# Where TensorE waits for u at the first down unit: one wait, or one per use

## The chip, the cores and the metric

One core of a Trainium2 chip runs the whole program. The metric is the device time of one execution in microseconds. The kernel before took 2634.83 us (median of 3 runs, 2634.37 to 2636.46).

## The reference

A streaming encoder trunk of two layers, for 512 prompt tokens and 32 sample tokens (544 columns in all), model width 1024. Each layer is FFN, middle part, FFN. What matters here is the FFN:

```
h = rmsnorm(x, norm_g[0]) * (1 + mod[:, 1]) + mod[:, 0]
x = x + 0.5 * mod[:, 2] * swiglu(h, w_up1, w_down1)

def swiglu(h, w_up, w_down):
    a, b = jnp.split(h @ w_up, 2, axis=-1)
    return (jax.nn.silu(a) * b) @ w_down          # w_up 1024 x 5632, w_down 2816 x 1024
```

Below, `u` is silu(a) * b. The middle part (pooling, retention, gates, output projection) is not touched. The vectors `mod` come from a product of the condition with `w_ada`, which the kernel spreads over the FFN stages.

## The kernel before, in words

**Data.** Everything is stored with features on the 128 partitions and the 544 tokens in the free dimension, cut into two column halves of HT = 272, called `hf` 0 and 1. Every fp32 operand is held as a rounded part and a remainder (`u_hi`, `u_lo`; `w_hi`, `w_lo`), and `product` (L447) makes a product out of three matmuls for each block of 128 rows: hi*hi, hi*lo and lo*hi, all summed in one PSUM bank.

**The FFN on TensorE** (`ffn`, L564) is cut into two halves of the 2816 hidden rows, HK = 11 blocks each. A half has 11 up units and then KD = 8 down units. There are two FFNs in each of two layers, so 8 halves. An up unit (`block_unit`, L484; `first_unit` for the first of a half 0) makes `a` and `b` of one block of u: for each `hf` it runs two products of 8 row blocks, 48 matmuls, 96 for the unit. A down unit makes 128 of the 1024 output features from the 11 blocks of u: for each `hf` one product with nk = 11, so 33 matmuls, 66 for the unit. Down unit n sums into the pair of PSUM banks n % 2.

**What follows an up unit.** When the last matmul of a `hf` ends, ScalarE applies Silu to `a` (L855), VectorE multiplies by `b` (L1189), and `two_parts` (L1030) rounds the result into `u_hi` (L1032) and stores the remainder in `u_lo` (L1034). The last of these raises the semaphore `u_ready` by 1, in the order block 0 hf 0, block 0 hf 1, block 1 hf 0, and so on: 22 rises in a half. The tally `u_t` counts them on TensorE's side.

**What TensorE waits for at a down unit.** `begin_unit` (L436) waits for `w_split`, the weights of the unit; `take` (L440) for the bank pair, `acc_free`; and ahead of the 8 down units of a half there is one wait for all 22 rises of `u_ready`:

```
place += 2 * HK
u_t.step(2 * HK)
pe.wait_ge(u_ready, u_t.at())
for n in range(KD):
    begin_unit()
```

**Weights.** SyncE loads the weights of a unit into one of two buffers `raw`, in order, once the buffer's previous content has been split (`w_split`). ScalarE rounds them into `w_hi` (L784) and VectorE forms `w_lo` (`split`, L1040). Both have two buffers as well, so ScalarE rounds the weights of unit m + 2 after unit m has ended on TensorE. In VectorE's order of work the split for down unit 0 stands ahead of both column halves of the last up unit, and the split for down unit 1 stands behind the u of hf 1 and behind one share of the `w_ada` work.

**The w_ada work.** While chunks of it are left, VectorE runs `due` after each column half of an up unit and after each down unit: four multiply-adds with `w_ada` rows (L1065), whose loads GpSimd's queue issues when a buffer comes free. Every fourth time TensorE sums the result in 16 small matmuls (`mods`, L497, L507). At the last block of a half this work is there in four of the 8 halves (both of the first FFN of layer 0, the first half of its second FFN and the first half of layer 1's first FFN).

**After a down unit** VectorE adds the result to x (`update_x`, L1154). In the second half of an FFN ScalarE then squares x for the next norm.

Of the kernel before, what the change touches and what calls it, by code (L numbers as in the profile page):

```python
# [20 lines left out]
HK = FF // P // 2  # L21
# [84 lines left out]
def trunk_kernel(nc, x_prompt, x_sample, c_prompt, c_sample, cache_pool, state_ret, w_ada, b_ada,  # L106
# [4 lines left out]
    with ctx:  # L111
        def sb(name, shape, dt=F32, stack=ctx):
            return stack.enter_context(nc.sbuf_tensor(name, [P, *shape], dt))

        def sem(name):
            return ctx.enter_context(nc.semaphore(name))
# [28 lines left out]
        with ExitStack() as st:  # L145
            u_hi, u_lo = sb("u_hi", [HK, T], F32R, st), sb("u_lo", [HK, T], F32R, st)
# [51 lines left out]
        u_ready = sem("u_ready")  # L198
# [230 lines left out]
        def _(pe):  # L429
            unit, ada, pair0, pair1, squares, h0, h1, u_t, tails, yp_t, mask_t, y_t, gn_t, side_t, layers = \  # L430
# [5 lines left out]
            def begin_unit():  # L436
                pe.wait_ge(w_split, unit.at(1))
                unit.step()

            def take(p):  # L440
                pe.wait_ge(acc_free[p], pairs[p].at(1))

            def done(p, ins):
                ins.then_inc(acc_ready[p], 1)
                pairs[p].step()

            def product(out, ws, xs, nk):  # L447


                for kk in range(nk):  # L450
                    for n, (a, b) in enumerate(((0, 0), (0, 1), (1, 0))):
                        last = mm(out, ws(a, kk), xs(b, kk), start=(kk == 0 and n == 0),  # L452
                                  stop=(kk == nk - 1 and n == 2))
                return last

            def cols(hf):
                return slice(hf * HT, (hf + 1) * HT)

            def parts(hi, lo, hf):
                return lambda b, kk: (hi, lo)[b][:, kk, cols(hf)]  # L460

            def w_view(p, pattern, n, **sizes):
                return [t[p][:, 0:n].rearrange(pattern, **sizes) for t in (w_hi, w_lo)]

            def first_unit(p, place=None):

                begin_unit()
                w = w_view(p, "p (b k n) -> p b k n", SLOT, b=2, k=KD)
                take(0)
                take(1)  # L470
                for kk in range(KD):
                    hs[kk % 2].step()
                    pe.wait_ge(h_ready[kk % 2], hs[kk % 2].at())
                    for hf in range(2):
                        for b in range(2):
                            for n, (c, d) in enumerate(((0, 0), (0, 1), (1, 0))):
                                last = mm(acc[:, 2 * hf + b, 0:HT], w[c][:, b, kk, :], (h_hi, h_lo)[d][:, kk, cols(hf)],  # L477
                                          start=(kk == 0 and n == 0), stop=(kk == KD - 1 and n == 2))
                        if kk == KD - 1:
                            done(hf, last)  # L480
                            if place is not None:
                                mods(place[0], place[1] + hf)

            def block_unit(p, place=None):  # L484

                begin_unit()
                w = w_view(p, "p (b k n) -> p b k n", SLOT, b=2, k=KD)
                for hf in range(2):
                    take(hf)
                    for b in range(2):  # L490
                        last = product(acc[:, 2 * hf + b, 0:HT], lambda a, kk: w[a][:, b, kk, :],
                                       parts(h_hi, h_lo, hf), KD)
                    done(hf, last)
                    if place is not None:
                        mods(place[0], place[1] + hf)

            def mods(todo, place):  # L497

                n, behind = divmod(place - LATE - 3, 4)
                if behind or not 0 <= n < len(todo):  # L500
                    return
                ada.step(4)
                pe.wait_ge(ada_used, ada.at())
                c = todo[n][1]
                for g in range(2):
                    for b in range(4):
                        last = mm(mod_cols(c // CHUNKS, (c % CHUNKS) * 4 + b, 1)[:, 0, g:g + 1],  # L507
                                  ada_acc[n % 2][:, g, b * P:(b + 1) * P], const[:, K_ONE:K_ONE + 1],
                                  start=True, stop=True)
                last.then_inc(mods_summed, 1)  # L510
# [45 lines left out]
            for layer in range(DEPTH):  # L556
                pe.matmul(ps_misc[:, layer * 192:layer * 192 + R_ALL], rows_in[0:R_ALL, layer, 0, :],
                          ident[0:R_ALL, 0:R_ALL], is_transpose=True, start=True, stop=True)
                n = R_CACHE + (2 * KD if layer == 0 else 0)
# [4 lines left out]
            def ffn(todo):  # L564
                for half in range(2):
                    place = half * (2 * HK + KD)
                    for n in range(HK):
                        if half == 0 and n == 0:
                            first_unit(0, (todo, place))
                        else:  # L570
                            block_unit((half + n) % 2, (todo, place + 2 * n))
                    place += 2 * HK
                    u_t.step(2 * HK)
                    pe.wait_ge(u_ready, u_t.at())
                    for n in range(KD):
                        begin_unit()
                        w = w_view((half + 1 + n) % 2, "p (k n) -> p k n", HK * P, k=HK)
                        take(n % 2)
                        for hf in range(2):
                            last = product(acc[:, 2 * (n % 2) + hf, 0:HT], lambda a, kk: w[a][:, kk, :],  # L580
                                           parts(u_hi, u_lo, hf), HK)
                        done(n % 2, last)
                        mods(todo, place + n)

# [65 lines left out]
            def middle():  # L650
                for kind, n in MID:
# [14 lines left out]
                    elif kind == "v":  # L666
                        begin_unit()
                        w = w_view(slot, "p (k n) -> p k n", SLOT, k=KD)
                        for t in range(TOK):
                            p = (n * TOK + t) % 2  # L670
                            rows = P if t < JB else TS
                            take(p)
                            done(p, product(acc[0:rows, 2 * p, 0:256],
                                            lambda a, kk: (h_hi, h_lo)[a][:, kk, t * P:t * P + rows],
                                            lambda b, kk: w[b][:, kk, :], KD))
                    elif kind == "map":
                        begin_unit()
                        w = w_view(slot, "p (g n) -> p g n", 2 * P, g=2)
                        for e in range(2):
                            g = 2 * n + e  # L680
                            yp_t.step()
                            pe.wait_ge(yp_ready, yp_t.at())
                            take(e)
                            for hf in range(2):
                                last = product(acc[:, 2 * e + hf, 0:HT], lambda a, kk: w[a][:, e, :],
                                               lambda b, kk: (yp_hi, yp_lo)[b][:, g, cols(hf)], 1)
                            done(e, last)
                    elif kind == "head":
                        head(n)
                    elif kind in ("mean", "var"):  # L690
                        group_sum()
# [36 lines left out]
            for layer in range(DEPTH):  # L728
                column_sums(KD)
                if layer == 0:  # L730
                    direct_rows()
                ffn(moved(layer, 0))
                column_sums(KD)
                middle()
                column_sums(KD)
                ffn(moved(layer, 2))
# [696 lines left out]
```

## Time and profile before

| | |
|---|---|
| median of 3 runs | 2634.83 us |
| the profiled execution, its own time | 2635.26 us |
| its span in the trace | 2633.4 us |
| mean granted TensorE clock | 0.977 |
| PE busy | 2478.3 us (94%), 19084 matmuls |
| DVE busy | 1473.5 us (56%) |
| ACT busy | 745.4 us (28%) |
| POOL busy | 241.6 us (9%) |
| HBM traffic | 105 GB/s over the span |

PE is TensorE's matmuls, PEld its weight loads (which overlap them), DVE is VectorE, ACT ScalarE, POOL GpSimd, SPq SyncE's DMA queue. Matmuls are pipelined: two that follow each other start about 0.125 us apart though each is shown with 0.29 us, so rates are read from starts and from stretches, not from the duration of one. PEclk is the granted TensorE clock as a share of 2.4 GHz: 1.00 is 2.4 GHz and 0.50 is 1.2 GHz.

### The profile page before, as it was taken

The page shows a single profiled execution, that of the slowest core. Times are in us where ns is not written, and L with a number is a line of the kernel's source. Part 1 is how long each engine was busy: PE and PEld are TensorE (multiplying, and loading weights), DVE is VectorE, ACT ScalarE, POOL GpSimd, SP SyncE. Part 2 cuts the span into 40 slices and gives each one's busy share as a digit, 9 for nine tenths or more (in the row PEclk, how much of TensorE's full clock was granted, in tenths as well). Part 3 has the DMA queues.
Part 4 walks back from the last instruction along what each step waited for, and adds up shares of the span by engine and source line. Part 5 has one row for each costly group of instructions (what it writes and reads, how often), then busy time and mean ns, then how long its engine had stood idle before and what let it go on. Part 6 is the DMA issues. An engine that isn't in the chain of part 4 may idle for free.

```text
span 2633.4 us, 42638 instructions
## 1 busy us (share of the span) xinstructions
PE 2478.3 (94%) x19084; PEld 2412.5 (92%) x19084; DVE 1473.5 (56%) x2229; ACT 745.4 (28%) x892; POOL 241.6 (9%) x232
## 2 busy tenths in 40 slices
PE   7899999898899899999989999998989998999997
PEld 2899999888799899999989999998879998999997
DVE  1876776645745577534367667645555545434333
ACT  2311222433422431222241122234233234212222
POOL 1210111101000221000021001011000002000001
PEclk9899999999999999999999999999999998999998
DMA  6554654311123355332245455332112323323321
GB/s 203 182 156 136 174 163 126 100 51 53 55 73 105 96 152 158 99 97 76 77 121 168 143 163 164 101 92 78 42 47 73 94 77 87 83 75 106 82 67 56
DMA packets 401157, 279.91 MB, mean 106 GB/s; under 512 B 10090, under 2 KB 379218, under 8 KB 400846
## 3 DMA queue, kind: packets, MB, share of 16 engines
q1 hardware_dynamic: 379027, 204.73, 27.5%
q0 software_dynamic: 18432, 67.12, 8.4%
q10 hardware_dynamic: 3515, 5.34, 0.6%
q8 instruction: 150, 2.46, 0.4%
q14 instruction: 33, 0.27, 0.0%
HBM read 273.74 MB, written 3.40 MB: 105 GB/s over the span
## 4 chain that ended last, share of the span: by engine, by line
PE 87%; DVE 6%; ACT 4%; issue 1%; DMA 1%; POOL 1%; ACTq 0%; POOLq 0%; DVEq 0%
PE acc L452 76%; PE acc L477 3%; PE ps_mod L507 2%; PE acc L720 2%; ACT w_hi L784 1%; DVE w_lo L1043 1%; DVE rstd L1118 1%; PE ps_sum L605 1%; DMA ada_raw<-in_w_ada 1%; POOL h_lo L383 1%; DVE rstd L1310 1%; ACT h_hi L797 0%; PE ps_sum L540 0%; DMA x_in<-in_x_sample 0%; DVE tmp L1127 0%
## 5 line engine op out<-in xcount | busy, mean ns | idle before, releaser
L452 PE MATMUL acc<-h_hi,w_hi 128*128 128x272 f32 x3648 | 1055.2, 289 | 9.5 <-DVE q L1301 3.6
L452 PE MATMUL acc<-h_lo,w_hi 128*128 128x272 f32 x3648 | 1051.8, 288 | 0.0
L452 PE MATMUL acc<-h_hi,w_lo 128*128 128x272 f32 x3648 | 1051.4, 288 | 0.0
L1043 DVE TENSOR_TENSOR w_lo<-raw,w_hi 128x2048 fp32r<-128x2048 f32 x224 | 512.7, 2289 | 358.6 <-ACT w_hi L784 358.5
L452 PEld LDWEIGHTS acc<-h_hi,w_hi 128*128 128x128 f32 x3648 | 688.5, 189 | 12.8 <-issue 12.0
L452 PEld LDWEIGHTS acc<-h_lo,w_hi 128*128 128x128 f32 x3648 | 688.3, 189 | 0.0
L452 PEld LDWEIGHTS acc<-h_hi,w_lo 128*128 128x128 f32 x3648 | 686.9, 188 | 0.0
L784 ACT ACTIVATE w_hi<-raw 128x2048 fp32r<-128x2048 f32 x224 | 427.7, 1909 | 333.1 <-PE acc L452 223.3
L452 PE MATMUL acc<-u_hi,w_hi 128*128 128x272 f32 x1408 | 407.4, 289 | 14.2 <-DVE u_lo L1034 14.2
L452 PE MATMUL acc<-u_lo,w_hi 128*128 128x272 f32 x1408 | 408.8, 290 | 0.0
L452 PE MATMUL acc<-u_hi,w_lo 128*128 128x272 f32 x1408 | 408.0, 290 | 0.0
L855 ACT ACTIVATE acted<-acc 128x272 f32<-128x272 f32 x176 | 70.0, 398 | 848.2 <-PE acc L452 839.6
L1065 DVE SCALAR_TENSOR_TENSOR ada_acc<-ada_raw,c_by,ada_acc 128x512 f32<-128x512 f32 x448 | 307.5, 745 | 0.1
L1189 DVE TENSOR_TENSOR prod<-acted,acc 128x272 f32<-128x272 f32 x176 | 76.8, 436 | 395.2 <-ACT acted L855 395.0
L452 PEld LDWEIGHTS acc<-u_hi,w_hi 128*128 128x128 f32 x1408 | 268.8, 191 | 15.9 <-DVE u_lo L1034 15.9
L452 PEld LDWEIGHTS acc<-u_hi,w_lo 128*128 128x128 f32 x1408 | 268.7, 191 | 0.0
L452 PEld LDWEIGHTS acc<-u_lo,w_hi 128*128 128x128 f32 x1408 | 268.2, 190 | 0.0
L383 POOL TENSOR_TENSOR h_lo<-tmp,h_hi 128x544 fp32r<-128x544 f32 x56 | 84.4, 1510 | 1332.7 <-ACT h_hi L797 1332.5
L1159 DVE SCALAR_TENSOR_TENSOR x<-acc,coef,x 128x272 f32<-128x272 f32 (+2 forms) x288 | 99.2, 400 | 182.6 <-PE acc L452 172.2
L411 POOL DMA_DIRECT2D ada_raw<-in_w_ada x128 | 92.6, 723 | 709.6 <-DVE ada_acc L1065 696.5
L477 PE MATMUL acc<-h_hi,w_hi 128*128 128x272 f32 x192 | 61.7, 321 | 54.1 <-DVE h_lo L1144 44.0
L796 ACT ACTIVATE tmp<-x 128x544 f32<-128x544 f32 x56 | 36.7, 656 | 220.4 <-issue 197.8
(171 smaller groups left out, 2507.8 us busy)
## 6 DMA issues: line engine op xcount, KB each, us to landing
raw<-in_w_up SPq DMA_DIRECT2D x176, 512.0 KB, 5.3
ada_raw<-in_w_ada POOLq DMA_DIRECT2D x128, 512.0 KB, 4.1
raw<-in_w_in SPq DMA_DIRECT2D x72, 512.0 KB, 4.6
raw<-in_w_down SPq DMA_DIRECT2D x64, 384.0 KB, 4.2
raw<-in_w_down SPq DMA_DIRECT2D x64, 320.0 KB, 3.4
ada_raw<-in_w_ada SPq DMA_DIRECT2D x16, 512.0 KB, 4.6
raw<-in_w_o SPq DMA_DIRECT2D x32, 256.0 KB, 2.9
raw<-in_w_pool_out SPq DMA_DIRECT2D x16, 256.0 KB, 3.0
```

The costliest lines, as they stand in the source:

```text
L383: pool.tensor_tensor(h_lo[:, n, :], tmp[:, n % 2, :], h_hi[:, n, :].bitcast(F32), ALU.subtract)\
L411: pool.dma_start(ada_raw[slot][:, :, :], ada_source(l, c, kp)).then_inc(ada_landed[slot], 16)
L452: last = mm(out, ws(a, kk), xs(b, kk), start=(kk == 0 and n == 0), stop=(kk == nk - 1 and n == 2))
L477: last = mm(acc[:, 2 * hf + b, 0:HT], w[c][:, b, kk, :], (h_hi, h_lo)[d][:, kk, cols(hf)], start=(kk == 0 and n == 0), stop=(kk == KD - 1 ...
L507: last = mm(mod_cols(c // CHUNKS, (c % CHUNKS) * 4 + b, 1)[:, 0, g:g + 1], ada_acc[n % 2][:, g, b * P:(b + 1) * P], const[:, K_ONE:K_ONE + 1],
L720: last = mm(acc[:, 2 * b + hf, 0:HT], w[c][:, kk, b * P:(b + 1) * P], (m_hi, m_lo)[d][:, kk, cols(hf)], start=(kk == 0 and n == 0), stop=( ...
L784: act.activation(w_hi[p][:, :], raw[p][:, :], ACT.Copy).then_inc(w_rounded, 1)
L855: act.activation(acted[:, hf, 0, :], acc[:, 2 * hf, 0:HT], ACT.Silu).then_inc(acted_ok, 1)
L1043: dve.tensor_tensor(w_lo[p][:, :], raw[p][:, :], f(w_hi[p][:, :]), ALU.subtract).then_inc(w_split, 1)
L1065: last = dve.scalar_tensor_tensor(to[:, g, :], ada_raw[slot][:, e, :], by, to[:, g, :], ALU.mult, ALU.add)
L1159: last = dve.scalar_tensor_tensor(x[:, n, c:c + b - a], acc[:, 2 * p + hf, a:b], coef[:, s, 2, n, g:g + 1], x[:, n, c:c + b - a], ALU.mult ...
L1189: dve.tensor_tensor(prod[:, hf, 0, :], acted[:, hf, 0, :], acc[:, 2 * hf + 1, 0:HT], ALU.mult).then_inc(acc_free[hf], 1)
```

## The change

The one wait ahead of the down units goes. In the first down unit of each half (n == 0), `product` is handed the base value of `u_ready` and waits twice itself: at its first row block for all blocks of u but the last, of its own column half, and at its last row block for that block. The other seven down units have no wait for u, before as after.

```
-            def product(out, ws, xs, nk):
+            def product(out, ws, xs, nk, ready=None):
                 for kk in range(nk):
+                    if ready is not None and kk in (0, nk - 1):
+                        pe.wait_ge(u_ready, ready + (2 * kk if kk else 2 * nk - 4))
                     for n, (a, b) in enumerate(((0, 0), (0, 1), (1, 0))):
                         last = mm(out, ws(a, kk), xs(b, kk), start=(kk == 0 and n == 0),
                                   stop=(kk == nk - 1 and n == 2))
...
                     place += 2 * HK
+                    u_first = u_t.at(1)
                     u_t.step(2 * HK)
-                    pe.wait_ge(u_ready, u_t.at())
                     for n in range(KD):
                         begin_unit()
...
                         for hf in range(2):
                             last = product(acc[:, 2 * (n % 2) + hf, 0:HT], lambda a, kk: w[a][:, kk, :],
-                                           parts(u_hi, u_lo, hf), HK)
+                                           parts(u_hi, u_lo, hf), HK,
+                                           u_first + hf if n == 0 else None)
```

With nk = 11 and hf the values waited for, counted from the half's first rise, are 19 + hf at the first row block (blocks 0 to 9 of that hf) and 21 + hf at the last. Each half has four waits for u in place of one.

## Rows read from the trace of the kernel before

**Rows 1.** Page, the chain that ended last: its shares by engine.
```profile
PE 87%; DVE 6%; ACT 4%; issue 1%; DMA 1%; POOL 1%; ACTq 0%; POOLq 0%; DVEq 0%
```

**Rows 2.** Waits of PE: engine line <- releaser: total us, times, longest us.
```profile
PE acc L477 <- DVE h_lo L1144: 44.0, 5, 10.0
PE acc L452 <- DVE u_lo L1034: 14.2, 8, 1.8
```

**Rows 3.** Chain in order of time, end of layer 0's second half: start, us, what.
```profile
434.01 0.41 ACT acted L855
...
435.24 0.45 DVE u_lo L1034
```

**Rows 4.** Timeline of PE, same place: start, us, instruction [idle <- releaser].
```profile
433.68 0.29 PE L452 MATMUL acc<-h_hi,w_lo 128*128 128x272 f32 x1
435.74 0.40 PE L452 MATMUL acc<-u_hi,w_hi 128*128 128x272 f32 x1 [1.77 <-DVE u_lo L1034]
```

**Rows 5.** Timeline of PE, the border of down units 0 and 1 of that half.
```profile
443.93 0.29 PE L452 MATMUL acc<-u_hi,w_lo 128*128 128x272 f32 x1
444.06 0.28 PE L452 MATMUL acc<-u_hi,w_hi 128*128 128x272 f32 x1
```

**Rows 6.** Timeline of PE, the change of column half inside an up unit.
```profile
304.50 0.30 PE L452 MATMUL acc<-h_lo,w_hi 128*128 128x272 f32 x1
304.64 0.28 PE L452 MATMUL acc<-h_hi,w_lo 128*128 128x272 f32 x1
```

**Rows 7.** Timeline of DVE around the same end of a half.
```profile
424.44 2.29 DVE L1043 TENSOR_TENSOR w_lo<-raw,w_hi 128x2048 fp32r<-128x2048 f32 x1
...
427.45 0.44 DVE L1034 TENSOR_TENSOR u_lo<-prod,u_hi 128x272 fp32r<-128x272 f32 x1
...
435.60 2.73 DVE L1065 SCALAR_TENSOR_TENSOR ada_acc<-ada_raw,c_by,ada_acc 128x512 f32<-128x512 f32 x4
438.25 2.29 DVE L1043 TENSOR_TENSOR w_lo<-raw,w_hi 128x2048 fp32r<-128x2048 f32 x1
```

**Rows 8.** Chain in order of time: down units of 66 matmuls, and `mods`.
```profile
219.77 10.02 PE acc L452 x66
...
1067.05 8.46 PE acc L452 x66
...
1110.08 1.68 PE ps_mod L507 x16
1111.76 8.31 PE acc L452 x66
```

**Rows 9.** Stretches behind starts of down unit 0 (seven of 8): us, PE busy, PEclk, DMA share, GB/s.
```profile
219.80:223.20 3.40, 3.40 (x16) 0.53 0.00 0
435.80:439.20 3.40, 3.40 (x27) 1.00 0.02 5
1067.10:1070.50 3.40, 3.40 (x27) 1.00 0.00 0
1271.30:1274.70 3.40, 3.40 (x18) 0.50 0.08 16
1496.60:1500.00 3.40, 3.40 (x17) 0.50 0.01 2
1712.30:1715.70 3.40, 3.40 (x27) 1.00 0.00 0
...
2537.60:2541.00 3.40, 3.40 (x18) 0.51 0.03 5
```

**Rows 10.** Eleven stretches of FFN without a stall: one of them, and their sum.
```profile
1075.00:1268.00 193.00, 193.00 (x1550) 1.00 0.32 88
...
sum 1486.80, PE 1485.66; mean PE 135.06
```

**Rows 11.** The middle part with its norm, layer 0 and layer 1.
```profile
519.80:922.90 403.10, 369.56 (x2788) 0.98 0.25 71
1791.60:2198.50 406.90, 374.26 (x2789) 0.96 0.24 70
```

More of the change, by code:

```diff
@@ L445, in done, with product @@
                 pairs[p].step()
-            def product(out, ws, xs, nk):
+            def product(out, ws, xs, nk, ready=None):
                 for kk in range(nk):
+                    if ready is not None and kk in (0, nk - 1):
+                        pe.wait_ge(u_ready, ready + (2 * kk if kk else 2 * nk - 4))
                     for n, (a, b) in enumerate(((0, 0), (0, 1), (1, 0))):
@@ L572, in ffn @@
                     place += 2 * HK
+                    u_first = u_t.at(1)
                     u_t.step(2 * HK)
-                    pe.wait_ge(u_ready, u_t.at())
                     for n in range(KD):
@@ L580, in ffn @@
                             last = product(acc[:, 2 * (n % 2) + hf, 0:HT], lambda a, kk: w[a][:, kk, :],
-                                           parts(u_hi, u_lo, hf), HK)
+                                           parts(u_hi, u_lo, hf), HK,
+                                           u_first + hf if n == 0 else None)
                         done(n % 2, last)
```

## The prediction

> **What bounds the kernel now.** I read the chain of waits first: PE holds 87% of it, with DVE 6% and ACT 4% far behind [rows 1]. In the FFN the chain is one long row of TensorE matmuls, so time is won there only where TensorE stands still or runs at the lower clock. The view of waits says where it stands still. The largest entry is the norm's (L477, 44.0 us, 5 times); the second is the one that this change is about: matmuls that wait for `u_lo`, 14.2 us in 8 waits, none above 1.8 us [rows 2]. Eight is the number of FFN halves, so each half pays it once, and all eight cost the same.
>
> The chain in order of time names what TensorE waits for at one of these places: Silu on ScalarE from 434.01, then product, rounding and remainder on VectorE, the last ending at 435.24 + 0.45 = 435.69 [rows 3]. That is the last block of u, hf 1, alone. Its matmuls are the last three of the 66 in the down unit, but the single wait holds all 66 for it.
>
> The third view is TensorE's own timeline: the last up matmul starts at 433.68, the first down matmul at 435.74 [rows 4]. From start to start that is 2.06 us.
>
> The fourth is the granted clock of the 3.4 us behind each restart. It is 0.50 to 0.53 (1.2 GHz) in five of the eight, and 1.00 (2.4 GHz) in three [rows 9]; of the five one is left out there, at 2336.3, which reads 0.50 as well. In eleven long stretches of the same matmuls without such a stall, 1486.8 us together, the clock column says 1.00 in every row; one is shown, with the sum [rows 10]. So the stall has a second price which the view of waits does not list.
>
> **The change part by part.**
>
> *The stall.* It goes if the new waits find their values there. The first unit then follows the last up unit as unit follows unit elsewhere: from 443.93 to 444.06, 0.13 us, across a border that holds two waits that were satisfied (weights and banks) [rows 5]. Saved per half: 2.06 - 0.13 = 1.93 us. Of this 1.77 is the idle time shown [rows 4]; the rest is the pipeline filling again (8.46 us for the 66 matmuls behind a stall against 8.31 for 66 without one, both at full clock [rows 8]). Eight halves: 15.4 us.
>
> *Are the values there?* Take the moment at which the first down matmul would start, 433.68 + 0.13 = 433.81. hf 0 wants blocks 0 to 9 first; at its last row block, 30 matmuls on (30 x 0.126 = 3.8 us, at 437.6), it wants block 10. VectorE stored the remainder of block 10, hf 0, from 427.45 to 427.89 [rows 7], ten microseconds ahead. hf 1 wants its blocks 0 to 9 at 433.81 + 33 x 0.126 = 438.0, and they are older still. Its block 10 is wanted 30 matmuls later, at 441.8, and stands at 435.69: 6 us to spare. What hides the 1.7 us of Silu and VectorE is 63 matmuls of the same unit. If that cover were gone the old stall would come back, no more.
>
> *The other waits at the head.* The weights of unit 0 were ready at 424.44 + 2.29 = 426.7, seven microseconds ahead [rows 7]. Bank pair 0 is freed by the product for hf 0 of the last up unit, ahead of the remainder at 427.45 [rows 7]. Cost nothing.
>
> *The clock.* 10.02 us against 8.46 for the same 66 matmuls, one behind a stall with the clock low, one behind a stall with it high [rows 8]: 1.56 us for each low stretch. Five of them: 7.8 us. Nothing in the new order stops TensorE there, so I take all five as gone. The bounds are 0 (they come anyway) and 7.8 us.
>
> The Trainium skill, page "TensorE: Matmul & The Clock Gate", section "HAM oscillation — how this bites in real kernels", speaks against this: it wants TensorE's idle gaps kept short, and the gaps that it warns of are longer than these of 1.77 us. By that page the eight stalls should not lower the clock, and the sum would be 15.4 us alone. The trace disagrees: five low stretches sit right behind five of them and none in the long stretches without a stall. I go by the trace and keep the page's outcome as a rival.
>
> *The added waits.* Four for one in each half, so 24 more in all, each satisfied when it is reached. The trace has satisfied waits in the same stream: at the unit's border 0.13 us [rows 5] and at the change of column half inside an up unit, where `take` waits, 304.50 to 304.64, 0.14 us [rows 6], against the usual 0.125. At most 0.015 us each, 0.4 us in all; I take 0. The far bound is a wait that stops the weight loads from running ahead, so that the pipeline fills anew; that is the 0.15 us worked out above, 24 x 0.15 = 3.6 us. A gain from a satisfied wait is excluded: it does no work.
>
> *What is late next.* Down unit 1. Its weights are split by VectorE behind the u of hf 1 (unchanged) and behind the `w_ada` share: 438.25 + 2.29 = 440.54 [rows 7]. It starts at 444.06 now [rows 5] and would start 1.93 earlier, at 442.13. The slack shrinks from 3.5 to 1.6 us and holds. This is the tightest kind of half: in the other three with `w_ada` work at this point 16 small matmuls follow unit 0, and in the four without it VectorE's 2.73 us of multiply-adds are absent or nearly so. Behind unit 1 everything on ScalarE, VectorE, SyncE's and GpSimd's queues hangs on the end of a TensorE unit as before, and moves with it. No instruction is queued behind a wait that it was not behind already: the only engine with changed waits is TensorE.
>
> *The rest of the program.* All that follows starts earlier by what was saved. Stalls remain (the norm, the retention), and which of them are followed by a low clock can change when the program shifts. The two middle parts do the same work and take 403.1 us with a mean clock of 0.98 and 406.9 us with 0.96 [rows 11]. I take this 3.8 us as the size of such an accident, to either side, and 0 as its mean. The same page of the skill says that the same kernel can see its clock change at different points in different runs; no run here shows that yet, and it changes no number.
>
> *Sum.* 15.4 + 7.8 = 23.2 us. The profiled execution took 2635.26 us (span 2633.4), so it would be 2612.1 (span 2610.2). The median of the runs is 0.4 us below the profiled execution, so the median after is 2634.8 - 23.2 = 2611.6 us, 0.88% less.
>
> **Rivals.**
>
> *The clock falls anyway.* If the low stretches come from something other than the stalls, only 15.4 us go: 2619.4 us. For it: three equal stalls have no low stretch behind them, and the page quoted. Against it: five of eight, and none in 1486.8 us without a stall. Chance 10%.
>
> *The added waits cost the loads' lead.* 3.6 us of the gain are lost: 2615.2 us. Against it are rows 5 and 6. Chance 3%.
>
> *The change does not do what it says*: another condition holds the head of the unit and takes the place of the wait removed, so that TensorE still stops for the same time: 2634.8 us. Against it: weights, banks and ten blocks of u have each been there for seven microseconds or more [rows 7]. Chance 2%.
>
> *Slower: the weights of down unit 1 take the wait's place.* In the four halves with `w_ada` work VectorE may have to wait for those rows in front of that split. This turns the gain only if it is very late: the slack is 1.6 us in one half and 1.6 + 1.7 = 3.3 in the three with 16 small matmuls behind unit 0 (1.68 us [rows 8]), 11.5 us together. With a delay of L in each the loss is 4L - 11.5, equal to the gain at L = 8.7 us; at L = 10 us it is 28.5 and the time 2640.1 us. Against it: the multiply-adds start at 435.60, with no idle time ahead of them, so the rows had landed [rows 7], and what loads them is released as before. Chance 2%.
>
> **How the numbers follow.** Forecast 83%, the clock stays 10%, load lead 3%, no effect 2%, slower 2%. Within the forecast the accident of the other stalls gives 2607.8 to 2615.4. The range is to leave out no more than 2 in 10: I take 2607 below (the accident, with a little of its own spread) and 2620 above, which holds the rivals of the clock and of the loads. The runs of before spread over 2.1 us, so a measurement can tell about 0.2% (5.3 us) from no change. Faster by more than that are the first three cases, 96%, less a little for an accident on top of them: 95%. Within it 3%, slower 2%.
>
> **What would show it.** In the changed kernel the waits of PE should have no entry for `u_lo` in matmuls on `w_hi` at down units, the chain at the end of a half should go from PE to PE with no Silu in it, and the first matmul on u should start 0.13 us behind the last up matmul. The remainder of block 10, hf 1, should be stored while PE is busy. The 3.4 us behind each of the eight borders should have the clock at 1.00 and 27 matmuls, and down unit 0 should take 8.3 us in all eight. Down unit 1 should start with no idle time, with its `w_lo` ended 1.6 us ahead in the tightest half. I am wrong on the clock if low stretches still stand at the borders, wrong on the accident if the middle parts differ from 403.1 and 406.9 us by more than 4 us, and wrong altogether if a wait for `w_lo` or for banks appears where `u_lo` was.

## The result and the profile after

The changed kernel took 2610.84 us (median of 4 runs, 2608.63 to 2611.30), the kernel before beside it 2635.45 us (4 runs, 2634.37 to 2636.46). The ratio is 0.9905 with a 95% interval from 0.9888 to 0.9922: 24.6 us less, where 23.2 was forecast; the time itself is 0.8 us from the predicted 2611.6. The profiled execution took 2611.3 us, its span 2609.5, 23.9 us shorter than before.

The view of waits of PE, after (L479 is the norm's line, L477 before). The entry for `u_lo`, second in [rows 2] with 14.2 us, is gone from the whole list; the norm's is unchanged to the digit.

```profile
PE acc L479 <- DVE h_lo L1147: 44.0, 5, 10.0
PE acc L553 <- DMA x_in<-in_x_sample: 12.1, 1, 12.1
PE acc L752 <- DVE x L1381: 11.4, 1, 11.4
```

The chain in order of time, after, from 427 to 448 us. In [rows 3] it left TensorE here for ScalarE and VectorE; now it is one piece of 169 matmuls.

```profile
426.98 21.03 PE acc L454 x169
```

The timeline of PE at the same border, the one of [rows 4], and at the border of down units 0 and 1 (to be held against [rows 5]). From the last up matmul to the first down matmul it is now 0.12 us from start to start, not 2.06, and unit 0 takes 438.14 - 429.94 = 8.20 us.

```profile
429.82 0.29 PE L454 MATMUL acc<-h_hi,w_lo 128*128 128x272 f32 x1
429.94 0.29 PE L454 MATMUL acc<-u_hi,w_hi 128*128 128x272 f32 x1
...
438.14 0.29 PE L454 MATMUL acc<-u_hi,w_hi 128*128 128x272 f32 x1
```

The timeline of DVE there, after, which answers to [rows 7]. The remainder of the last block of u is stored at 431.82, while TensorE works; the weights of unit 1 end at 436.67, 1.47 us before that unit starts (1.6 forecast).

```profile
431.38 0.44 DVE L1037 TENSOR_TENSOR u_lo<-prod,u_hi 128x272 fp32r<-128x272 f32 x1
431.74 2.73 DVE L1068 SCALAR_TENSOR_TENSOR ada_acc<-ada_raw,c_by,ada_acc 128x512 f32<-128x512 f32 x4
434.39 2.28 DVE L1046 TENSOR_TENSOR w_lo<-raw,w_hi 128x2048 fp32r<-128x2048 f32 x1
...
438.35 1.04 DVE L1162 SCALAR_TENSOR_TENSOR x<-acc,coef,x 128x272 f32<-128x272 f32 x3 [1.68 <-PE acc L454]
```

The stretches behind the eight borders, after, two of the eight (us, PE busy, PEclk, DMA share, GB/s). All eight have the clock at 1.00. Before, five of the eight were at 0.50 to 0.53 (four of them in [rows 9], the fifth at 2336.3 us).

```profile
217.60:221.00 3.40, 3.40 (x29) 1.00 0.39 140
...
1265.30:1268.70 3.40, 3.40 (x30) 1.00 0.00 0
```

**Where the 23.9 us went.** Borders, from start to start: 8 x (2.06 - 0.13) = 15.4 us. The first unit, start to start of its 66 matmuls: 8.30 us behind a stall at full clock, 8.20 without one, 8 x 0.10 = 0.8 us. The five low stretches: 9.86 against 8.30 us for the unit, 5 x 1.56 = 7.8 us. Together 24.0. The two middle parts, which the change does not touch, took 810.0 us together before [rows 11] and 810.3 after, but with the roles exchanged: the layer that took 407 us now took 403, and the other way round (same columns):

```profile
513.90:921.10 407.20, 374.42 (x2789) 0.96 0.25 70
1778.90:2182.00 403.10, 369.49 (x2789) 0.98 0.25 71
```

### The profile page after: what moved, and what is told of

It reads as the page before. It is cut to its first block, busy times and chain, and to the rows that moved or that the text cites. A ratio compares the mean times of both kernels' runs of the same rounds, so it can differ in the third digit from the quotient of the medians.

```text
span 2609.5 us, 42638 instructions
## 1 busy us (share of the span) xinstructions
PE 2468.1 (95%) x19084; PEld 2403.4 (92%) x19084; DVE 1474.1 (56%) x2229; ACT 745.4 (29%) x892; POOL 241.8 (9%) x232
## 4 chain that ended last, share of the span: by engine, by line
PE 87%; DVE 6%; ACT 4%; issue 1%; DMA 1%; POOL 1%; ACTq 0%; POOLq 0%; DVEq 0%
PE acc L454 76%; PE acc L479 3%; PE ps_mod L509 2%; PE acc L723 2%; ACT w_hi L787 1%; DVE w_lo L1046 1%; PE ps_sum L608 1%; DVE rstd L1121 1%; DMA ada_raw<-in_w_ada 1%; POOL h_lo L383 1%; DVE rstd L1313 1%; ACT h_hi L800 0%; DMA x_in<-in_x_sample 0%; PE ps_sum L542 0%; DVE tmp L1130 0%
## 5 line engine op out<-in xcount | busy, mean ns | idle before, releaser
L454 PE MATMUL acc<-u_lo,w_hi 128*128 128x272 f32 x1408 | 404.8, 287 | 0.0
L454 PE MATMUL acc<-u_hi,w_hi 128*128 128x272 f32 x1408 | 403.1, 286 | 0.0
L479 PE MATMUL acc<-h_hi,w_hi 128*128 128x272 f32 x192 | 61.9, 322 | 54.1 <-DVE h_lo L1147 44.0
```

## The experiments

Twelve runs follow: ten changed kernels, the kernel before once more and the change once more. They were measured in four groups, each on a chip of its own and with the kernel before beside it (2637.61, 2637.26, 2636.75 and 2636.43 us; single runs from 2632.39 to 2642.44). Ratios are to the kernel before of the same group; where I compare with the change (2610.84 us) instead, the two were mostly measured on different chips.

### Filling the stall instead of removing it

Rival to be told apart: the low clock has a cause of its own, and its 7.8 us are no part of the stall's price. The edit, on the kernel before (the wait ahead of the loop goes, and stands behind the filling instead):

```
                         take(n % 2)
+                        if n == 0:
+                            for _ in range(14):
+                                mm(acc[:, 0, 0:HT], ones[:, :], w_hi[(half + 1) % 2][:, 0:HT], start=True, stop=True)
+                            pe.wait_ge(u_ready, u_t.at())
```

> The kernel before, with 14 idle matmuls of full size put where TensorE stands still (behind the wait for weights and banks, ahead of the wait for all of u; their result is overwritten). They fill some 1.76 of the 1.93 us, so the down units start when they did. My theory (the stall lowers the clock behind it, at 1.56 us for each low stretch, five of them): no low clock behind the borders, 7.8 us less than before, about 2627.5 us. Rival (the low stretches come from something else, or the median execution has none): 2635 us, unchanged. If the refilling of the pipeline (0.15 us each) is saved too, about 2626.5 us.

Measured: 2631.82 us (11 runs, 2629.14 to 2632.29) against 2637.61; ratio 0.9976 (0.9967 to 0.9985), so 4.0 to 8.7 us less. The timeline of PE at the border of layer 0's second half shows the filling (L580) in the place of the stall, and that u comes no earlier: from the last up matmul to the first down matmul it is still 432.71 - 430.65 = 2.06 us.

```profile
430.65 0.29 PE L452 MATMUL acc<-h_hi,w_lo 128*128 128x272 f32 x1
430.78 1.93 PE L580 MATMUL acc<-w_hi,ones 128*128 128x272 f32 x14
432.71 0.39 PE L452 MATMUL acc<-u_hi,w_hi 128*128 128x272 f32 x1
```

The stretches behind the borders, two of eight; every one of the eight reads 1.00:

```profile
218.30:221.70 3.40, 3.40 (x27) 1.00 0.00 0
...
2533.50:2536.90 3.40, 3.40 (x27) 1.00 0.00 0
```

The rival is out: with the same wait, the same start of the down units and idle work in between, the low stretches are gone. All eight first units take 8.30 to 8.33 us. The forecast of 7.8 us less lies in the interval, the median says 5.8. How many low stretches the other runs of the kernel before had is not known. The profiled execution's span, 2628.3 us, is 5.1 us below the first profile of before and 10.0 below the second (next experiment); its middle parts took 406.7 and 407.3 us against 403.1 and 406.9 in the first [rows 11], so that the other stalls took back some of the 7.8. The pipeline's refilling (8.30, not 8.20) was not saved.

### The kernel before, profiled again

> The kernel before, unchanged, for a second profile of it. My theory: each of the eight stalls is there again with 2.06 us from start to start, and a number of low stretches behind them that need not be five nor at the same borders, 1.55 us each, which is where the 7 us of spread of this kernel come from. Rival: five again, at the same borders.

Measured: one run, 2640.07 us, span 2638.3. Eight stalls of 2.06 us each, and again five low stretches, but not at the same borders: the first of [rows 9] was low and is high here, the second the reverse; the third is low now, the fourth high.

```profile
218.60:222.00 3.40, 3.40 (x27) 1.00 0.00 0
433.00:436.40 3.40, 3.40 (x16) 0.52 0.02 5
1071.20:1074.60 3.40, 3.40 (x16) 0.53 0.00 0
1276.20:1279.60 3.40, 3.40 (x27) 1.00 0.02 5
```

In all the five read 0.52 to 0.61. So which stall is followed by a low clock varies from execution to execution. The number was five in both, which two profiles cannot make a rule of. The 4.8 us by which this execution was slower than the first are mostly in the middle parts: from first matmul behind the norm to first matmul behind the next one 408.0 and 407.3 us, against 403.1 and 406.9 [rows 11].

### A longer stall

On VectorE, for the last block, hf 1:

```
+                            if n == HK - 1 and hf == 1:
+                                split(half)
                             two_parts(u_hi[:, n, cols(hf)], u_lo[:, n, cols(hf)], prod[:, hf, 0, :], u_ready)
                             due(todo, place + 2 * n + hf)
                     place += 2 * HK
-                    split(half)
```

> The kernel before with a longer stall: VectorE splits the weights of down unit 1 ahead of rounding the last block of u, so that u comes some 3.6 us later and the stall is 5.5 us from start to start. My theory: 8 x 3.6 = 28.6 us more, and a low stretch behind all eight borders in place of five, 4.7 us more: about 2668 us. Rival (the clock has nothing to do with the stall): 2664 us and five or so low stretches.

Measured: 2671.92 us (2671.06 to 2672.24) against 2637.61, ratio 1.0130 (1.0116 to 1.0144), 34.3 us more where 33.3 was expected. The rival without a share of the clock said 2664. The waits of PE:

```profile
PE acc L452 <- DVE u_lo L1034: 43.0, 8, 5.4
```

All eight stretches behind the borders are low, two shown:

```profile
442.20:445.60 3.40, 3.40 (x15) 0.50 0.78 217
...
1079.80:1083.20 3.40, 3.40 (x18) 0.60 0.72 212
```

Five of eight behind 2.06 us, eight of eight behind 5.66 us from start to start. The unit 0 behind them takes 9.6 to 11.0 us, so that some low stretches cost more than 1.56 us: the low clock lasts 6.8 us around six of these borders (from 440.8 to 447.6 at one) and 3.4 us around the other two.

### The same late u under the cover

The same edit of VectorE, on the changed kernel.

> The change together with the order of VectorE that made u 3.6 us later in the kernel before (the split for down unit 1 ahead of rounding the last block of u). My theory: block 10 of hf 1 is stored 5.6 us after the last up matmul starts and wanted at 8.0 us, so 63 matmuls still cover it: no wait, no low clock at the borders, 2611 us as the change. Rival (the cover holds only for the 1.9 us of the original chain, or down unit 1 comes late): some of the 28.6 us comes back, 2615 to 2640 us.

Measured: 2610.90 us (2609.80 to 2612.32), ratio 0.9900 (0.9887 to 0.9914): nothing comes back. The timeline of DVE shows u stored at 435.12, 5.6 us behind the start of the last up matmul at 429.5; it is wanted 63 matmuls behind the border, near 437.5.

```profile
432.14 2.29 DVE L1046 TENSOR_TENSOR w_lo<-raw,w_hi 128x2048 fp32r<-128x2048 f32 x1 [1.43 <-ACT w_hi L787]
434.36 0.29 DVE L1035 CAST u_hi<-prod 128x272 fp32r<-128x272 f32 x1
434.68 0.44 DVE L1037 TENSOR_TENSOR u_lo<-prod,u_hi 128x272 fp32r<-128x272 f32 x1
```

One edit, 34.3 us without the cover and none with it.

### A part of the cover

The wait for all 22 rises at row block 2 of hf 0, six matmuls into the unit:

```
-                    if ready is not None and kk in (0, nk - 1):
-                        pe.wait_ge(u_ready, ready + (2 * kk if kk else 2 * nk - 4))
+                    if ready is not None and kk in (0, 2):
+                        pe.wait_ge(u_ready, ready + 2 * nk - (1 if kk else 4))
...
-                                           u_first + hf if n == 0 else None)
+                                           u_first if n == 0 and hf == 0 else None)
```

> A part of the cover: the head waits for all but the last row block, and the wait for all 22 rises stands at row block 2 of hf 0, six matmuls (0.75 us) on. TensorE stops for 1.93 - 0.75 = 1.18 us longer than its pace, 9.4 us in eight halves: 2620.3 us if so short a stop never lowers the clock, 2628 us if it does so five times. My theory says that the clock's share falls with the length of the stop; I expect two low stretches, 2623 us, and a wait for u_lo of about 1.0 us each.

Measured: 2625.58 us (5 runs, 2624.94 to 2625.95), ratio 0.9955 (0.9943 to 0.9968). The waits are 8.2 us in 8, one of them on the timeline of PE here:

```profile
430.88 0.29 PE L454 MATMUL acc<-u_hi,w_lo 128*128 128x272 f32 x1
432.19 0.39 PE L454 MATMUL acc<-u_hi,w_hi 128*128 128x272 f32 x1 [1.02 <-DVE u_lo L1037]
```

Unit 0 takes 9.48 to 9.51 us at all eight borders, 1.3 us more than 8.20, eight times 10.4. The clock is 1.00 throughout all eight units: I had expected two low stretches, and there is none. The rest of the 14.7 us over the change is in the middle parts: 408.0 and 406.8 us here, 407.2 and 403.1 in the changed kernel's profile. The median lies above the 2623 us expected, and above the 2620.3 us for no low stretch at the borders.

### The change in one half of each FFN

```
                     u_t.step(2 * HK)
+                    if half:
+                        pe.wait_ge(u_ready, u_t.at())
```

> The change in the first half of each FFN only; in the second half the one wait for all of u stands again. My theory: four stalls come back at 1.93 us and 0.10 us for the slower refilling of the first unit, 8.1 us, and two or three of them lower the clock at 1.55 us: 2622 to 2624 us, half of the way. Rival (one kind of half carries the gain): 2611 or 2635 us.

Measured: 2620.38 us (5 runs, 2619.54 to 2622.68), ratio 0.9936 (0.9922 to 0.9949). In its profile the four borders of second halves have 2.06 us again, two of them with a low clock, and the four others 0.13 us. 4 x 2.03 + 2 x 1.55 = 11.2 us, and its span is 2620.9, 11.4 us above the changed kernel's 2609.5. In the profile the prices add up border by border; the median of the runs is 1.6 us below the range that I gave.

### Division by column half alone

```
-                    if ready is not None and kk in (0, nk - 1):
-                        pe.wait_ge(u_ready, ready + (2 * kk if kk else 2 * nk - 4))
+                    if ready is not None and kk == 0:
+                        pe.wait_ge(u_ready, ready + 2 * (nk - 1))
```

> The change with the wait divided by column half only: at the head of each product of the first down unit one wait for all 11 blocks of its own half, none at the last row block. My theory: block 10 of hf 0 is stored some 6 us before the unit starts and block 10 of hf 1 about 1.9 us after, while its product starts at 4.2 us, so nothing waits: 2610.8 us, as the change. Rival (it is the division by row block that hides the chain): the wait comes back in part, up to 15 us, 2626 us.

Measured: 2611.05 us (2609.67 to 2611.44), ratio 0.9899 (0.9884 to 0.9914): as the change. No wait for `u_lo` in the list, and the border at 0.12 us:

```profile
429.31 0.29 PE L454 MATMUL acc<-h_hi,w_lo 128*128 128x272 f32 x1
429.43 0.29 PE L454 MATMUL acc<-u_hi,w_hi 128*128 128x272 f32 x1
```

What hides the chain is that hf 1 waits for itself. The further division at the last row block adds room (hf 1's block is wanted at 7.9 us behind the border, not at 4.2) but no time here.

### A wait at every row block

```
-            def product(out, ws, xs, nk, ready=None):
+            def product(out, ws, xs, nk, ready=None, first=False):
...
-                    if ready is not None and kk in (0, nk - 1):
-                        pe.wait_ge(u_ready, ready + (2 * kk if kk else 2 * nk - 4))
+                    if ready is not None:
+                        pe.wait_ge(u_ready, ready + 2 * (kk if kk else (nk - 2 if first else 0)))
...
-                                           u_first + hf if n == 0 else None)
+                                           u_first + hf, n == 0)
```

> The change with a wait for u at every row block of every down unit, 1376 waits more, all satisfied when reached. My theory (a satisfied wait is free): 2610.8 us. The bound from the change of column half, 0.015 us each: 2631 us. The far bound, a pipeline that fills anew at 0.15 us each: over 2800 us.

Measured: 2611.24 us (2610.21 to 2613.98), ratio 0.9902 (0.9889 to 0.9916). 1376 satisfied waits more cost 0.4 us by the medians, nothing that can be measured: even 3 us would be 0.002 us each. On the same chip the kernel with one wait per column half took 2611.05. The 0.015 us that I read out of one change of column half [rows 6] was too much.

### Filling the norm's stall

If a filled stall keeps the clock up, the norm's stalls of 8 to 10 us look like the next gain. On the changed kernel, at the head of `first_unit`:

```
+            firsts = []
+
             def first_unit(p, place=None):
...
+                if firsts:
+                    for _ in range(56):
+                        mm(acc[:, 0, 0:HT], ones[:, :], w_hi[p][:, 0:HT], start=True, stop=True)
+                firsts.append(0)
                 for kk in range(KD):
```

> The change, with the means of the first experiment used at another stall: 56 idle matmuls (7.0 us at full clock) ahead of the first unit behind each norm but the very first, where TensorE stands still for 8.2 to 10.3 us. Now the first 24 matmuls of that unit take 4.7 to 5.6 us against 3.0 at full clock. My theory: the filled stall keeps the clock up and gives back about 2 us at each of five norms: 2601 us. Rival (the clock is down already from the sparse column sums ahead of it, so that the filling takes 12 us and holds the unit up): 2615 to 2625 us.

Measured: 2612.76 us (2611.36 to 2614.26), ratio 0.9908 (0.9893 to 0.9923). No gain over the change (2610.90 for the late u under the cover, on the same chip), though the mean clock rose from 0.979 to 0.987. The stretch from the end of the column sums in layer 0's second FFN to the end of the first unit, of the filled kernel and then of the changed one:

```profile
1335.30:1358.60 23.30, 21.23 (x154) 0.93 0.18 48
```

```profile
1335.30:1358.80 23.50, 14.26 (x98) 0.78 0.19 49
```

0.2 us are won where the clock went from 0.78 to 0.93. In the chain the unit starts when VectorE's part of h comes, which is at the same time in both; again the filled kernel first:

```profile
1343.84 0.84 DVE h_lo L1153 x2
1344.67 0.04 issue
1344.72 13.46 PE acc L485 x90
```

```profile
1344.81 13.60 PE acc L479 x90
```

At this norm the unit itself was hardly faster clocked: its filling ended 2.07 us before h came, and the clock fell again from 1346.15 to 1349.56, inside the unit. The norm ahead of layer 1's middle part is the clean case. There the unit has the clock at 1.00 in the filled kernel and at 0.86 in the changed one, and takes as long:

```profile
1778.60:1792.60 14.00, 13.56 (x96) 1.00 0.00 1
```

```profile
1778.90:1792.80 13.90, 13.90 (x96) 0.86 0.00 1
```

The chain shows what holds it. In the changed kernel it stays on TensorE for all 96 matmuls; in the filled one it passes through VectorE, ScalarE and GpSimd, which make h row block by row block, and comes back for the last 36:

```profile
1785.97 1.70 POOL h_lo L376
1787.67 0.04 issue
1787.71 3.27 PE acc L485 x24
```

```profile
1778.88 14.09 PE acc L479 x96
```

Neither theory held. The filling did not hold the unit up. The first 24 matmuls, from which I had reckoned 2 us, are slow at the low clock, but GpSimd stores its remainder of the last row block of h 12.26 us into this unit in the changed kernel and 12.38 in the filled one, so a faster start only meets a longer wait. Over the five norms the units did get shorter, 68.2 us in place of 70.6 from first to last matmul; the two middle parts took 408.3 and 405.0 us in place of 407.2 and 403.1, which used that up.

### Filling four stalls of the middle part

In the middle parts equal work took 403 or 407 us. On the changed kernel, with `idle(out, k)` for k idle matmuls of 272 columns:

```
+                if hd == 0:
+                    idle(ps_sum[:, 1, 0:HT], 19)
                 values(0)
...
+                            if n and not e:
+                                idle(ps_misc[:, 0:HT], 17)
                             pe.wait_ge(yp_ready, yp_t.at())
...
+                        if (kind, n) == ("var", HEADS - 1):
+                            idle(ps_misc[:, 0:HT], 11)
                         group_sum()
+                idle(ps_misc[:, 0:HT], 13)
```

> The change, with idle matmuls in four stalls of each middle part (19 ahead of the first values product of head 0, 17 ahead of the map of groups 2 and 3, 11 ahead of the last variance, 13 behind it), where TensorE stops for 2.8, 2.5, 1.6 and 1.8 us from start to start. Theory: the 4 us by which equal middle parts differ are low stretches behind those stalls, where TensorE sets the pace of what follows; filled, both middle parts take 403 us or less: 2605 to 2608 us. Rival (as at the norm, another engine sets the pace there): 2611 us; if a filling is longer than its stall: up to 2614 us.

Measured: 2606.47 us (2605.42 to 2607.82), ratio 0.9884 (0.9870 to 0.9897). The stretch of layer 0's middle part around the start of the long gate stage that TensorE bounds, in the changed kernel and in this one (186 and 184 us into the part; 41 of the 108 matmuls are fillings):

```profile
700.00:715.00 15.00, 10.28 (x49) 0.66 0.33 92
```

```profile
697.00:712.00 15.00, 14.21 (x108) 1.00 0.26 70
```

The middle parts of this kernel take 404.8 and 402.2 us, against 407.2 and 403.1, so that layer 0's missed the 403 us of the theory:

```profile
513.10:917.90 404.80, 378.65 (x2848) 0.97 0.25 70
1775.10:2177.30 402.20, 374.39 (x2849) 0.99 0.25 71
```

The traces without fillings show where the 4 us lie. Layer 0's part, first in the kernel before (403.1 us) and then in the changed one (407.2 us), 10.2 us near the start of the gate stage:

```profile
711.50:721.70 10.20, 9.65 (x66) 0.83 0.55 154
```

```profile
704.30:714.50 10.20, 7.66 (x34) 0.50 0.44 122
```

The gate stage begins at 712.05, 192.2 us into the part, and has the low clock for 2.9 us; in the changed kernel it begins at 708.67, 194.8 us into it, and has the low clock for 5.9 us. So 2.5 of the 4.1 us are lost ahead of the gate stage and the rest behind its start. The other profiles of kernels with these stalls unfilled agree: parts of 403.1 to 403.3 us have two low stretches of 3.4 us between the norm and the next one, parts of 406.7 us and more have one of 10.2 us and at least one of 3.4; three parts of 404.8 to 405.0 us lie between. In the filled kernel layer 1's part has none, layer 0's has two of 3.4 us (617.5 and 675.6) and still took 404.8.

### The change again, and the fillings with the simpler wait

> The change, unchanged, on the same chip as the next run, so that the two can be compared. My theory: 2611 us, a spread of some 3 us, no low stretch at the eight borders again.

> The four fillings of the middle part together with the wait divided by column half. My theory: both are worth here what they were worth alone, so 2606.5 us, 4 to 5 us below the change on the same chip. Rival (the 4 us were an accident of the other chip): 2611 us.

Measured on one chip: the change 2610.86 us (2608.61 to 2612.00), ratio 0.9901 (0.9884 to 0.9917); the fillings with the wait by column half 2607.82 us (2606.77 to 2609.97), ratio 0.9892 (0.9878 to 0.9907). The fillings win 3.0 us by the medians, less than the 4 to 5 that I expected, and the two ranges overlap. Taken over both kernels with fillings, eight runs lie between 2605.42 and 2609.97; three kernels that do the change's work without them (the change, the change again, by column half) have twelve between 2608.61 and 2612.00. The changed kernel's profile here has middle parts of 407.2 and 403.3 us, the filled one's 405.4 and 402.7. A gain of 3 to 4 us is likely and not secured; these are the fastest kernels of the study.

## Why the prediction was right

**The stall.** 1.93 us a border from start to start, 15.4 in eight: measured the same. One piece of the working was wrong. I said that the 0.15 us of refilling were part of the 1.93. The refilling comes on top of it, inside unit 0, and is 0.10 us from start to start (8.30 against 8.20): 0.8 us in all that the sum left out.

**The clock.** 1.56 us for each low stretch, five of them: 9.86 against 8.30 us in the profile before. This term was disputed, and the first experiment carries it: the wait kept, the clock's fall gone. The rival that the clock falls anyway (2619.4 us) is refuted by it. A stop of 2.06 us (start to start) lowered the clock in twelve of twenty cases, over three profiles, one of 5.66 us in eight of eight, one of 1.3 us in none of eight. The Trainium skill, page "TensorE: Matmul & The Clock Gate", section "HAM oscillation — how this bites in real kernels", warns only of longer gaps than this one; the traces disagree, and they decide. The second profile of the kernel before shows other borders low than the first. The Trainium skill, same page, section "What's actually happening", says that the cold start of one kernel varies from run to run; the traces agree in so far as the same stops differ between two executions. The number five was read from one execution; that it was five again in a second, and that the median of the runs fitted it, was in part luck, since two profiles do not fix it.

**The values at the head.** Right for all but one thing that I did not see: hf 0 needs no division at all, since its last block was stored 5.9 us before the unit would start (427.89 against 433.81). The division by column half carries the whole gain, and the row blocks none.

**The added waits.** Taken as 0, measured as 0; the far bound of 3.6 us is out.

**What is late next.** The slack of down unit 1 in the tightest half was forecast as 1.6 us and is 1.47; it held, so the slower rival (2640 us) never began.

**The accident of the other stalls.** Named as 3.8 us to either side. The two parts exchanged their times, so that it came to 0.3 us between the two profiled executions; that was luck. Against the second profile of the kernel before (408.0 and 407.3 us) it is 5.0 us, more than I had allowed. My own sign of being wrong here was a middle part that moves by more than 4 us, and layer 0's moved by 4.1: the term was too small. It shows up again where another kernel missed its forecast by a few us: the wait at row block 2 (one middle part at 406.8 in place of 403.1 us), and the second profile of the kernel before. What causes the two values was shown only in part: they go with the low stretches around the gate stage, and with four of the stalls filled the clock there is up and the parts are 2.4 and 0.9 us shorter. Four profiles of kernels without a stall at the borders (the change twice, the wait by column half, the late u) have the same two values in the same layers, 407.2 and 403.1 to 403.3, so it is not mere chance there; a fifth, with a wait at every row block, has 407.9 and 404.8. What decides which stalls are hit stays open.

**The size of the error.** 24.6 us measured with an interval of about 4.5 us to either side, 23.2 forecast, 24.0 by the terms as measured in the two profiled executions. The interval is wider than the refilling and the accident, so the medians alone could not have told them from nothing.

## What to carry to other kernels

A wait ahead of a unit should ask for what its first instruction needs, not for what its last one does; one split of a wait by the order in which the values come (here: by column half) is enough, if the work ahead of the late value is longer than the chain that makes it. Price a stall of TensorE with what follows it: look at the granted clock behind the restart, since here a third of the gain lay there and the view of waits does not list it. A low clock costs time only where TensorE sets the pace; behind the norm ahead of layer 1's middle part, where h comes from VectorE and GpSimd, raising it from 0.86 to 1.00 gave nothing.

## What the runs showed of the hardware

- Behind a stop of TensorE of 2.06 us from start to start the granted clock fell to half (1.2 GHz) for 3.4 us in twelve of twenty cases; which stops are hit varies between executions of the same kernel (five of eight borders in each of two profiles, not the same five). Each such stretch cost 1.56 us. With 14 idle matmuls in the stop it happened in none of eight.
- A satisfied wait ahead of a matmul cost nothing that could be measured: 1376 of them, 0.4 us by the medians.
- Behind a stop the next 66 matmuls took 0.10 us longer at full clock, whether the stop was empty or filled with other matmuls (8.29 to 8.33 us in both, 8.20 without a wait that blocks).
- The kernel before varied by 7.6 us from run to run on one chip (2633.07 to 2640.62 in 15 runs), with the stalls filled by 3.2 us on the same chip (2629.14 to 2632.29 in 11). Whether the change itself narrows the scatter is not shown: on the one chip where both were run side by side, the kernel before varied by 1.7 us in seven runs and the changed one by 3.4 in four.
